# Seven block products for eight in the gate and up tiles of four feed-forward blocks

## What is computed

```
def _swiglu(h, w_gate_up, w_down):
    g, u = jnp.split(h @ w_gate_up, 2, axis=-1)      # 1024 -> 2 x 2816
    return (jax.nn.silu(g) * u) @ w_down             # 2816 -> 1024

for layer in range(2):
    x = x + 0.5 * _swiglu(_rmsnorm(x, ffn1_norm[layer]), ffn1_w_gate_up[layer], ffn1_w_down[layer])
    x = x + _hybrid_mixer(_rmsnorm(x, mix_norm[layer]), w_in[layer], ..., w_out[layer], ...)
    x = x + 0.5 * _swiglu(_rmsnorm(x, ffn2_norm[layer]), ffn2_w_gate_up[layer], ffn2_w_down[layer])
```

## Time and profile before

| | us |
|---|---|
| median of three runs | 3470.36 (3468.59 to 3473.2) |
| span of the profiled execution | 3469.3 |
| PE busy | 3386.1 |
| POOL busy | 1476.8 |
| DVE busy | 1265.4 |
| ACT busy | 1248.9 |

### The profile page before, as it was taken

One profiled execution on the slowest core, in us unless ns is written; L12 is line 12 of the kernel. 1 busy time (PEld: TensorE's weight loads), 2 busy tenths in 40 slices (PEclk: granted clock), 3 DMA queues, 4 the chain that ended last, 5 costly groups with the idle time before them and its releaser, 6 DMA issues.

```text
span 3469.3 us, 38407 instructions
## 1 busy us (share of the span) xinstructions
PE 3386.1 (98%) x15598; PEld 2714.4 (78%) x15598; DVE 1265.4 (36%) x2298; ACT 1248.9 (36%) x1988; POOL 1476.8 (43%) x674
## 2 busy tenths in 40 slices
PE   8999999998999999999999999999999999999998
PEld 5767788887888888887677888888887778888776
DVE  3266775523221144212663111111123652111555
ACT  4533323533222232223554222322224653222543
POOL 4323445654444444445414444444436234444332
PEclk8999999999999999999999999999999999999999
DMA  7211333442333323434213333233333123333221
GB/s 274 69 52 61 98 97 124 156 140 73 125 125 127 99 96 134 141 96 113 70 37 99 96 96 96 91 103 96 95 105 106 38 77 97 97 92 103 73 61 55
DMA packets 102174, 345.40 MB, mean 100 GB/s; under 512 B 12173, under 2 KB 12557, under 8 KB 101838
## 3 DMA queue, kind: packets, MB, share of 16 engines
q1 hardware_dynamic: 101200, 341.10, 31.1%
q10 hardware_dynamic: 798, 1.85, 0.1%
HBM read 336.08 MB, written 2.10 MB: 97 GB/s over the span
## 4 chain that ended last, share of the span: by engine, by line
PE 89%; DVE 4%; ACT 3%; DMA 1%; issue 1%; POOL 1%; SPq 0%; ACTq 0%; DVEq 0%
PE ps L1200 25%; PE ps L1202 25%; PE ps L1201 25%; PE ps L1231 2%; PE ps L1232 2%; PE ps L1233 2%; PE ps L1501 2%; PE ps L1528 1%; PE ps L1511 1%; POOL t L2673 1%; DMA t<-in_w_f1i 1%; PE ps L1420 1%; PE ps L1434 0%; DVE t L2101 0%; PE ps L1289 0%
## 5 line engine op out<-in xcount | busy, mean ns | idle before, releaser
L2673 POOL TENSOR_TENSOR t<-t,t 128x1024 fp32r<-128x1024 f32 (+2 forms) x584 | 1355.7, 2323 | 1884.1 <-ACT t L1586 1875.6
L1200 PE MATMUL ps<-t,t 128*128 128x512 f32 x4016 | 1596.1, 397 | 19.9 <-POOL t L2673 13.7
L1202 PE MATMUL ps<-t,t 128*128 128x512 f32 x4016 | 1571.3, 391 | 0.0
L1201 PE MATMUL ps<-t,t 128*128 128x512 f32 x4016 | 1566.8, 390 | 0.0
L1200 PEld LDWEIGHTS ps<-t,t 128*128 128x128 f32 x4016 | 757.1, 189 | 198.4 <-issue 27.3
L1202 PEld LDWEIGHTS ps<-t,t 128*128 128x128 f32 x4016 | 756.2, 188 | 166.3
L1201 PEld LDWEIGHTS ps<-t,t 128*128 128x128 f32 x4016 | 757.2, 189 | 156.9 <-issue 1.7
L1586 ACT CAST t<-t 128x1024 fp32r<-128x1024 f32 (+2 forms) x588 | 584.2, 995 | 584.4 <-PE ps L1202 419.7
L2446 DVE TENSOR_TENSOR t<-t,ps 128x512 f32<-128x512 f32 x110 | 75.7, 688 | 529.9 <-PE ps L1202 513.8
L1652 ACT CAST t<-t 128x512 fp32r<-128x512 f32 x158 | 97.2, 622 | 403.3 <-DVE t L2446 355.2
L1845 ACT ACTIVATE t<-t 128x512 f32<-128x512 f32 x88 | 55.6, 632 | 314.1 <-DVE t L2439 314.0
(11 more groups left out here) (293 smaller groups left out, 2246.4 us busy)
## 6 DMA issues: line engine op xcount, KB each, us to landing
t<-in_w_f1i SPq DMA_DIRECT2D x88, 512.0 KB, 3.6
t<-in_w_f2i SPq DMA_DIRECT2D x88, 512.0 KB, 3.5
t<-in_w_ada SPq DMA_DIRECT2D x72, 512.0 KB, 4.5
t<-in_w_ffi SPq DMA_DIRECT2D x44, 512.0 KB, 4.0
t<-in_w_f1o SPq DMA_DIRECT2D x32, 512.0 KB, 3.5
t<-in_w_f2o SPq DMA_DIRECT2D x32, 512.0 KB, 3.5
t<-in_w_gate SPq DMA_DIRECT2D x24, 512.0 KB, 4.2
t<-in_w_out SPq DMA_DIRECT2D x48, 256.0 KB, 2.6
```

The costliest lines, as they stand in the source:

```text
L1200: e.matmul(out, wh[:, at], X.hi[c][:, 0:N], start=c == first, stop=False)
L1201: e.matmul(out, wh[:, at], X.lo[c][:, 0:N], start=False, stop=False)
L1202: m = e.matmul(out, wl[:, at], X.hi[c][:, 0:N], start=False, stop=c == final)
L2673: e.tensor_tensor(k.WL[:, n % NHL, 0:w], k.raw[:, j % NRAW, 0:w], f(k.WH[:, n % NHL, 0:w]), ALU.subtract).then_inc(*k.rest.inc(('rest', j) ...
```

## The change

In f1_0, f2_0, f1_1 and f2_1 a gate tile and an up tile are made as one 2 by 2 block product. The weight blocks A11, A12 (gate) and A21, A22 (up) are the even and the odd contraction tiles, the token blocks b are even or odd contraction tiles by 256 tokens of either half. Seven products of sums replace eight: each is 4 contraction steps of three matmuls over 256 tokens (`product`). DVE forms the weight sums S1 and S2 in a PSUM bank and S3 and S4 in SBUF (`sums`), ACT rounds the seven pieces (`round`), POOL takes five of the low parts and DVE two (`minus`). The products are added up by `first_copy`, `second_sum`, `third_sum`, `up_sum` and `last_sum`; p2 adds to the bank of p1, p3 to the bank of p5. The pieces of pair i+1 are made during pair i. The seven token blocks are made where x is updated (`sum_parts`, `sum_lows`, `last_lows`), so `residual` of ff1 and f2_0 and of out2 grows.

All five blocks run their pairs in two parts, 14 and 8 middle tiles, with a down pass of 14 tiles after the first (`partial` adds it to x) and one of 8 after the second. That makes room for the token blocks. The modulation steps run two per pair in ff1 and none in f1_0. The squares' sum of x ahead of f2 is taken by POOL and no longer by DVE in a bank.

```diff
-NRAW, NHL, LOOK, LEAD = (5, 3, 2, 2)
+NRAW, LOOK, LEAD = (5, 2, 2)
+PARTS = ((0, 14), (14, 8))
+PIECES = ('A11', 'S1', 'S2', 'S3', 'A22', 'A12', 'S4')
+PRODUCTS = {'p1': ('A11', 'b11', 'A', 0), 'p5': ('S1', 't1', 'D', 256), 'p6': ('S2', 't2', 'B', 0), 'p7': ('S3', 't3', 'C', 0), 'p4': ('A22', 't4', 'D', 0), 'p2': ('A12', 'b21', 'A', 0), 'p3': ('S4', 'b22', 'D', 256)}
...
 def ffn(on, k, m):
+    for part, (first, count) in enumerate(PARTS):
+        (plain if m.scale is None else fours)(on, m, first, count)
+        after = (m.next, 0) if part else (None if m.scale is None else m, first + count)
+        for n in range(KT):
+            if after[0] is not None:
+                begin_pair(on, *after, n)
+            on.T(('ed'[part], m.tag, n), m.wo, n, m.mid, kt=count, first=first)
+            if part:
+                on.residual(m.res, n, ('d', m.tag, n), ('filled', ('u', m.tag, FF - 1)))
+            else:
+                on.partial(m.res, n, ('e', m.tag, n))
+
+
+def begin_pair(on, m, i, n):
+
+    if n == KT - 2:
+        on.sums(m, i, 'S1')
+        on.round(m, i, 'A11')
+        on.round(m, i, 'S1')
+        on.minus(m, i, 'A11')
+        on.minus(m, i, 'S1')
+        on.sums(m, i, 'S2')
+        on.round(m, i, 'S2')
+    if n == KT - 1:
+        on.sums(m, i, 'S3')
+        on.minus(m, i, 'S2')
+        on.round(m, i, 'S3')
+        on.minus(m, i, 'S3')
+
+
...
+        for _ in range(2 if i > 2 else 0):
+            next(m.side, None)
...
+def fours(on, m, first, count):
+
+    final = first + count - 1
+    for i in range(first, first + count):
+        on.pair(m, i)
+        begin, more = (i == first, i < final)
+        on.product(m, i, 'p1')
+        if not begin:
+            on.last_sum(m, i - 1)
+            if i > 1:
+                on.pair_gate(m, i - 1)
+        on.first_copy(m, i)
+        if begin:
+            on.round(m, i, 'A22')
+            on.minus(m, i, 'A22')
+            on.sums(m, i, 'S4')
+            on.round(m, i, 'A12')
+            on.round(m, i, 'S4')
+            on.minus(m, i, 'A12')
+            on.minus(m, i, 'S4')
+        if more:
+            on.round(m, i + 1, 'A11')
+            on.minus(m, i + 1, 'A11')
+        on.product(m, i, 'p5')
+        if i == 1:
             on.row(m.scale)
-            on.ffn_gate(m, 0)
-            on.ffn_up(m, 0)
-            on.ffn_gate(m, 1)
-        if m.scale is None or i > 0:
-            on.ffn_up(m, i)
+            on.pair_gate(m, 0)
+        if more:
+            on.sums(m, i + 1, 'S1')
+            on.round(m, i + 1, 'S1')
+        if not begin:
+            on.pair_up(m, i - 1)
+        if more:
+            on.minus(m, i + 1, 'S1')
+            on.sums(m, i + 1, 'S2')
+            on.round(m, i + 1, 'S2')
+        if i == 0:
+            for j in m.before.later:
+                on.last_lows(m.before, j)
+            for j in range(4):
+                on.product(m, i, 'p6', (j,))
+                on.product(m, i, 'p7', (j,))
+        else:
+            on.product(m, i, 'p6')
+        if not begin:
+            on.mid_low(m, i - 1)
+        on.second_sum(m, i)
+        if i:
+            on.product(m, i, 'p7')
+        if more:
+            on.sums(m, i + 1, 'S3')
+            on.round(m, i + 1, 'S3')
+            on.minus(m, i + 1, 'S3')
+        else:
+            on.early(2)
+        on.third_sum(m, i)
+        on.product(m, i, 'p4')
+        if more:
+            on.round(m, i + 1, 'A22')
+            on.minus(m, i + 1, 'A22')
+            on.minus(m, i + 1, 'S2')
+        on.up_sum(m, i)
+        on.product(m, i, 'p2')
+        if i == 0:
+            on.roots(m.scale, 4 if m.whole else 2)
+        if more:
+            on.round(m, i + 1, 'A12')
+            on.minus(m, i + 1, 'A12')
+            on.sums(m, i + 1, 'S4')
+            on.round(m, i + 1, 'S4')
+            on.minus(m, i + 1, 'S4')
+        on.product(m, i, 'p3')
         if m.whole is not None and i == 2:
+            on.roots(m.whole.sum, 1)
+        if m.whole is not None and i == 3:
             on.row(m.whole.sum)
-        if m.whole is not None and 3 <= i < 11:
-            on.final_tile(m.whole, i - 3, 'final_g')
-        if i > 2:
-            next(m.side, None)
-    for n in range(KT):
-        on.T(('d', m.tag, n), m.wo, n, m.mid, kt=FF)
...
+    def product(self, m, i, p, js=range(4), start=True):
+
+        k, e = (self.k, self.e)
+        piece, x, bank, col = PRODUCTS[p]
+        wh, wl = (piece_at(k, k.WH, m, i, piece), piece_at(k, k.WL, m, i, piece))
+        key = (bank, m.tag, i)
+        opens = p in ('p1', 'p5', 'p6', 'p7')
+        out = (self.take(k.banks, *key, hold=i == 0 and bank == 'A') if opens and js[0] == 0 else self.bank(*key))[:, col:col + 256]
+        if i == 1 and p == 'p6':
+            k.banks.let(('A', m.tag, 0))
+        self.wait_ge('rest', m.tag, i, piece)
+        if p == 'p2':
+            self.wait_ge('first copy', m.tag, i)
+        if p == 'p3':
+            self.wait_ge('up sum', m.tag, i)
+        for j in js:
+            at = slice(128 * j, 128 * j + 128)
+            self.wait_ge('lo', m.A.tag, j, x)
+            e.matmul(out, wh[:, at], m.A.hi(j, x), start=opens and j == 0, stop=False, skip_group_check=not opens)
+            e.matmul(out, wh[:, at], m.A.lo(j, x), start=False, stop=False, skip_group_check=not opens)
+            mm = e.matmul(out, wl[:, at], m.A.hi(j, x), start=False, stop=j == 3, skip_group_check=not opens)
+        if js[-1] == 3:
+            mm.then_inc(*k.filled.inc(('used', m.tag, i, piece), ('filled', (p, m.tag, i)), *([('filled', ('u', m.tag, i))] if p == 'p3' else [])))
+
...
+    def up_sum(self, m, i):
+
+        k, e = (self.k, self.e)
+        two = lambda ap: ap.rearrange('p (a n) -> p a n', n=256)
+        self.wait_ge('filled', ('p4', m.tag, i))
+        self.wait_ge('third sum', m.tag, i)
+        e.tensor_tensor(two(self.bank('C', m.tag, i)), two(self.bank('D', m.tag, i)), two(k.tmp[3][:, 256:512]).broadcast_to([128, 2, 256]), ALU.add).then_inc(*k.dve.inc(('up sum', m.tag, i)))
...
+    def sum_parts(self, event, A, n, g):
+
+        k, e, j, x, b = (self.k, self.e, n // 2, self.k.X[:, n, :], self.bank('G', A.tag, n // 2))
+        one, two = (b[:, 0:256], b[:, 256:512])
+        if n % 2 == 0:
+            self.wait_ge('x scaled', A.tag, j)
+            self.wait_ge('hi', A.tag, j, 'b11')
+            e.tensor_tensor(A.lo(j, 'b11'), one, f(A.hi(j, 'b11')), ALU.subtract).then_inc(*k.dve.inc(('lo', A.tag, j, 'b11')))
+            e.scalar_tensor_tensor(one, x[:, 256:512], g, one, ALU.mult, ALU.subtract).then_inc(*k.dve.inc(('x sum', A.tag, j, 't1')))
+        else:
+            self.wait_ge(*event)
+            self.wait_ge('lo', A.tag, j, 't1')
+            e.scalar_tensor_tensor(one, x[:, 256:512], g, one, ALU.mult, ALU.subtract).then_inc(*k.dve.inc(('x sum', A.tag, j, 't2')))
+            e.scalar_tensor_tensor(two, x[:, 256:512], g, two, ALU.mult, ALU.subtract).then_inc(*k.dve.inc())
+            self.lent('H', A.tag, j)
+            self.wait_ge('x sum', A.tag, j, 't2')
+            e.scalar_tensor_tensor(self.bank('H', A.tag, j)[:, 0:256], x[:, 0:256], g, one, ALU.mult, ALU.subtract).then_inc(*k.dve.inc(('x sum', A.tag, j, 't4')))
...
+    def sum_lows(self, A, n):
+
+        k, e, j, b = (self.k, self.e, n // 2, self.bank('G', A.tag, n // 2))
+        if n % 2 == 0:
+            self.wait_ge('hi', A.tag, j, 't1')
+            e.tensor_tensor(A.lo(j, 't1'), b[:, 0:256], f(A.hi(j, 't1')), ALU.subtract).then_inc(*k.dve.inc(('lo', A.tag, j, 't1')))
+        else:
+            self.wait_ge('hi', A.tag, j, 't2')
+            e.tensor_tensor(A.lo(j, 't2', 2), b, f(A.hi(j, 't2', 2)), ALU.subtract).then_inc(*k.dve.inc(('lo', A.tag, j, 't2'), ('lo', A.tag, j, 't3'), ('free', ('G', A.tag, j))))
+            self.wait_ge('hi', A.tag, j, 't4')
+            e.tensor_tensor(A.lo(j, 't4'), self.bank('H', A.tag, j)[:, 0:256], f(A.hi(j, 't4')), ALU.subtract).then_inc(*k.dve.inc(('lo', A.tag, j, 't4'), ('free', ('H', A.tag, j))))
+
```

315 lines of the change are left out of this document (261 added, 54 removed).

## The result

The changed kernel takes 3531.73 us (median of four runs, 3526.55 to 3537.78) against 3471.78 us for the kernel before on the same chip: a ratio of 1.017, 95% interval 1.0151 to 1.0190. The profiled execution has a span of 3531.1 us, 61.8 above that of before. The forecast was 3466 with a range of 3415 to 3500: the time lies outside it, on the slower side, to which I had given a chance of 0.38.

What follows compares the result with a forecast made beforehand. The prediction took PE, busy 3386.1 of 3469.3 us, as the bound. It set 88.9 us less in the pairs against added costs, mostly at joints, for -4.6 us, and forecast 3466 us, range 3415 to 3500.

Steps and rivals of the forecast that it cites:

- The gain on PE: Gate and up pairs: 84 matmuls of 256 columns take 9.87 us instead of 10.88, 88.9 us less over 88 pairs.
- the walk of DVE's list: Inside a pair: up sum ends at 8.1 us, p3 would start at 8.46, so the loop holds with 0.3 to spare.
- The slow rival: In the pairs, DVE becomes the bound, at the up sum ahead of p3: 3497 us, chance 0.25.
- the weight load: Rival: weight loads bound the pairs at 14.6 us each, 3800 us in all, chance 0.03.
- (e): ff1, two modulation loads a pair: every other pair of 15 waits about 2 us, 15 us, bounds 3 and 30.
- The partial down pass: Down pass of 14 tiles: put at nothing, since an output has 9.6 us of cover.
- (a) to (d): Joints: starts of f1_0 and f1_1 15.7 and 12.4 us, both f2 27.6, pair 1 9.6, pair 14 3.
- the clock: Starts of f1_0 and f1_1: after PE's gap the clock is low, 1.2 GHz, which costs 2.5 to 3 us.
- (c): Pair 1 of each block: gate waits for the row, up sum at 11.7 where 9.4 is needed, 9.6 us.
- Term (d): Pair 14: roundings of five pieces stand ahead of S1 on ACT, 3 us.
- The fast rival: Joints overlap better than walked and the gain is kept: 3418 us, chance 0.20.
- (f): Eight final tiles of three SBUF operands lie in DVE's tight loop: 1 us.

Runs made afterwards that it cites:

- e11_short: Changed kernel with product p7 cut to one contraction step of four in every pair but the first of each block; 3485.47 us.
- e2_pieces: Changed kernel with the first pieces of pair 14 issued behind outputs 6 and 7 of the first down pass, not ahead; 3504.03 us.
- e6_hold: Changed kernel with bank C, of pair 0's up product, held out of the turn until p3 of pair 1; 3529.00 us.
- e5_banks: Changed kernel with the same two PSUM banks held for the token blocks through a whole pass; 3531.20 us.
- e8_skew: Changed kernel with modulation steps respread, pair 14's pieces later, own token-block banks, bank C held, roots and row earlier, DVE updating the next output first; 3470.91 us.
- e10_joints_skew: As e8_skew, plus weight sums' bank held, first copy later, late low parts earlier, modulation steps moved, DVE's new order only for outputs 0 to 5; 3474.48 us.
- e14_twice: Changed kernel with DVE's low part of token block t4 made three times, with a wait between; 3537.37 us.

## Why the prediction was wrong, step by step

- **The gain on PE** held: 81.8 of 88.9 us, and 4.8 that I had not counted. Rows of 256-column matmuls priced it, with a small slip: 15 steps in 1.76 us are 0.1173 us apiece and not 0.1175, and the pairs ran at 0.1184. So did **the walk of DVE's list**: up sum at 8.1 forecast and found, 0.3 us of room forecast and 0.5 found by `e11_short`. The slow rival's mechanism, DVE as the bound in the pairs, did not happen, though its 3497 was nearer; nor was the weight load the bound.
- **(e), the modulation steps of ff1**, 15 us with bounds 3 and 30: 38 measured. The chain load, rounding, low part was right. The step that failed is "With another 1.28 us, or 2.1 with the port" and, behind it, "Every other pair of the 15 waits about 2". A step that meets a subtraction does not cost 0.8 us more but 2.0 to 2.1, and in ff1 half of them met one, at times both of a pair (6.76 us). The load behind them landed after 5.1 to 5.9 us and not 4.0. Why the steps meet POOL so often was not tested; in the row above their delay had bunched three subtractions. The rule of the Trainium skill (SBUF — State Buffer, SBUF: two separate sides) is that of the two engines the one that starts first has the shared ports for its whole instruction, and the other stands. The trace agrees: each of the 14 long steps ended 1.08 us after one subtraction. I priced the rule for a part of an instruction, and for one step of the two.
- **"The partial down pass ... I put at nothing"**: 26 us, shown by `e2_pieces`. I had checked the cover of x's update and not the steps that `begin_pair` places ahead of an output: a rounding that waits for a weight buffer holds the next output's weights behind it on ACT. The same steps ahead of a last pass, with one weight unit per output, made outputs 6 and 7 of ff1 only 1.1 and 1.2 us later than the like ones before them.
- **The joints**, (a) to (d), 68.3 forecast: 88.8 measured. The mechanism held. The bank of p5 and S4 were where the walk had them: S4 ended some 60 us after the pass began (58 walked), and PE stood 12.3 us (4.9 in output 7 and 7.4 at p5) where I had 13, and 7.3 to 8 us in the first pairs of the other three where I had 8 to 11. The step that failed is the clock, "which costs 2.5 to 3 us", counted once for each f1: the gap is several shorter waits, with stretches of lower clock behind them that took about 28 us in the four joints. The rest of the error is small. The wait for POOL in the first two odd outputs of a last pass was 1.6 us each, 3.2 a pass where I had 1. (c) was 2.4 each; PE stood 3.85 for the middle tile's bank, with the up sum's 2.1 just under it, as `e6_hold` showed. Term (d) was not measured by itself.
- **The fast rival**, joints of 35 us, was refuted by the joints measured, 88.8 us; `e5_banks`, `e8_skew` and `e10_joints_skew` add that neither own banks nor the looser order on DVE give them back.

Of the 66 us of error, 23 lie in (e), 26 in the down pass, 20.5 in the joints and 2 in the pairs; 4 came back in the first attention stage. Term (f), 1 us, does not show: pairs of f1_0 with a final tile beside them took 9.84 to 9.86 us. By my own signs, joints over 50 us and pairs under 10.1, the forecast would have stood: what broke it lay largely where I had named no sign. The modulations and the down pass alone would have made 3515 us, outside the range.

## What to carry to other kernels

A gain spread thinly over many iterations (1 us in 11) is paid for at every joint, and the joints are where extra work on the small engines has no cover: price them output by output, and each step that is placed ahead of a wait by what stands behind it in its queue. When two steps are moved into one slot, walk two slots, since the first delay changes what the second meets. Side work is cheap only beside the long stretches: the same step was nearly free next to a 9.6 us output and cost 3 us next to one that already fed the next block. And count what follows a wait with it: three waits of 4 to 7 us brought 6 us more at the lower clock.

## What the runs showed of the hardware

An operation of DVE with SBUF operands alone that starts beside a POOL subtraction ends a fixed time after it: 1.08 us for the modulation steps, 0.55 for the low part of b2. In ff1 such steps took 3.23 to 3.42 us instead of 1.28, and four low parts of 0.75 us took 6.22 beside four subtractions; none waited for more than one subtraction, and the subtractions grew too, from 1.28 to 1.7 us in the last case. The mean over the 49 modulation steps was 2.24 us here and 1.75 in the kernel before. Such an operation also acts as a barrier that swallows delays ahead of it, as `e14_twice` showed. An operation with one operand in PSUM kept its length beside a busy POOL (L2850 at 919.88, 0.69 us). Groups by line of the changed kernel, modulation steps, then the low part of b2:

```profile
L2451 DVE SCALAR_TENSOR_TENSOR t<-t,t,t 128x1024 f32<-128x1024 f32 x49 | 109.5, 2235 | 36.8 <-DMA t<-in_w_ada 35.1
...
L2775 DVE SCALAR_TENSOR_TENSOR t<-t,t,t 128x512 fp32r<-128x512 f32 x16 | 20.7, 1325 | 0.0
```

In the first joint PE's granted clock was 0.50 for 3.4 to 4.84 us behind each wait of 3.85 to 7.40 us. It did not always fall: after 3.07 us of waiting it was 0.50 in the kernel before and 1.00 in the changed one, at the same place.
